# Hybrid attention block on one core: sparse value products from whole 32-bit operands, with three edits in the order of work beside them

## What is computed

```python
score = jnp.einsum('bqhs,bqh->bqs', jax.nn.relu(logits), wb)      # indexer, 4 heads
_, sel = lax.top_k(score, topk)                                    # 256 of the keys
sc = jnp.einsum('bqhd,bqkd->bhqk', qb, kg) * (dh ** -0.5)          # 8 heads of 64, one shared key head
p = jax.nn.softmax(sc, axis=-1)
return jnp.einsum('bhqk,bqkd->bqhd', p, vg)                        # the value products
```

## Time and profile before

| | |
|---|---|
| median of 3 runs | 2812.31 us (2811.92 to 2814.73) |
| the profiled execution | 2818.59 us, its span 2816.8 us |
| PE busy | 2528.1 us, 90% of the span, 13093 matmuls |
| DVE busy | 1786.0 us, 63% |
| ACT busy | 1372.1 us, 49% |
| POOL busy | 410.3 us, 15% |
| mean granted clock of PE | 0.972 of full speed |

### The profile page before, as it was taken

The page is one execution under the profiler, slowest core; times in us unless marked ns, Lnnn a source line. Parts: engine busy times, 40 slices in busy tenths (PEclk is TensorE's granted clock), DMA queues, the critical chain, the costliest instruction groups (busy, mean ns, idle before and its releaser), DMA issues.

```text
span 2816.8 us, 37280 instructions
## 1 busy us (share of the span) xinstructions
PE 2528.1 (90%) x13093; PEld 2095.4 (74%) x13093; DVE 1786.0 (63%) x3597; ACT 1372.1 (49%) x2768; POOL 410.3 (15%) x397
## 2 busy tenths in 40 slices
PE   5998999998999999999898999999878888878896
PEld 4776888776778888877677778887667777667785
DVE  6466676225767687227778878622778887777522
ACT  4455645344646444216657445522665673454511
POOL 5334353440000000100000000010000001000010
PEclk9999999999999999999999999999999999999998
DMA  5756584785343522664343511166324333000154
GB/s 162 227 176 213 170 282 150 252 278 183 115 162 119 173 76 68 209 209 155 115 143 104 165 60 53 46 217 206 137 83 149 105 108 132 23 31 31 38 179 165
DMA packets 172537, 399.36 MB, mean 142 GB/s; under 512 B 13760, under 2 KB 96704, under 8 KB 162368
## 3 DMA queue, kind: packets, MB, share of 16 engines
q1 hardware_dynamic: 172352, 396.96, 42.8%
HBM read 308.31 MB, written 88.60 MB: 141 GB/s over the span
## 4 chain that ended last, share of the span: by engine, by line
PE 51%; DVE 21%; ACT 15%; issue 10%; DMA 1%; POOL 1%; SPq 0%; DVEq 0%; ACTq 0%; POOLq 0%
PE bank L861 38%; PE TR L760 5%; PE PV L828 5%; ACT signs L1026 4%; ACT prob L991 3%; ACT prob L1001 3%; DVE ptL L1396 2%; ACT ptH L1015 2%; DVE prob L1355 2%; DVE nmx L1365 2%; DVE score L1617 2%; DVE zs L1427 1%; PE bank L771 1%; PE bank L772 1%; DVE flags L1543 1%
## 5 line engine op out<-in xcount | busy, mean ns | idle before, releaser
L861 PE MATMUL bank<-hH,pairs 128*128 128x512 f32 (+1 forms) x3584 | 1158.5, 393 | 21.0 <-DVE zs L1459 7.6
L861 PEld LDWEIGHTS bank<-hH,pairs 128*128 128x128 f32 x3584 | 679.3, 191 | 160.6 <-issue 22.2
L861 PE MATMUL bank<-hL,pairs 128*128 128x512 f32 (+2 forms) x1792 | 704.1, 393 | 0.0
L1026 ACT ACTIVATE signs<-score,bits 128x384 int8<-128x384 f32 (+7 forms) x256 | 335.8, 1312 | 214.5 <-DVE bits L1497 201.5
L1396 DVE TENSOR_TENSOR ptL<-TR,ptH 128x512 fp32r<-128x512 f32 (+1 forms) x384 | 256.9, 670 | 260.1 <-ACT ptH L1015 256.9
L861 PEld LDWEIGHTS bank<-hL,pairs 128*128 128x128 f32 (+1 forms) x1792 | 343.3, 192 | 65.2
L1015 ACT ACTIVATE ptH<-TR 128x512 fp32r<-128x512 f32 (+1 forms) x384 | 219.6, 576 | 333.6 <-PE TR L760 332.6
L1478 DVE TENSOR_SCALAR_CACHE_REDUCE above<-score,bits 128x256 uint8<-128x256 f32 (+10 forms) x280 | 348.1, 1243 | 9.5
L760 PE MATMUL TR<-identR,prob 128*128 128x128 f32 x1480 | 232.6, 279 | 101.0 <-ACT prob L1001 53.2
L760 PEld LDWEIGHTS TR<-identR,prob 128*128 128x128 f32 x1480 | 178.1, 142 | 178.4 <-ACT prob L1001 66.9
L1176 POOL TENSOR_TENSOR pairs<-raw,pairs 128x512 fp32r<-128x512 f32 x164 | 218.1, 1339 | 316.1 <-ACT pairs L960 315.9
(11 more groups left out here) (206 smaller groups left out, 3636.1 us busy)
## 6 DMA issues: line engine op xcount, KB each, us to landing
pairs<-w_split SPq DMA_DIRECT2D x444, 512.0 KB, 3.5
w_split<-pairs SPq DMA_DIRECT2D x74, 1024.0 KB, 4.9
raw<-in_w_in SPq DMA_DIRECT2D x106, 256.0 KB, 5.6
xs<-in_x SPq DMA_DIRECT2D x4, 2048.0 KB, 9.2
rows<-in_x SPq DMA_DIRECT2D x16, 512.0 KB, 5.2
out<-rows SPq DMA_DIRECT2D x4, 2048.0 KB, 7.5
table<-trig SPq DMA_DIRECT2D x48, 128.0 KB, 2.8
raw<-in_w_branch SPq DMA_DIRECT2D x24, 256.0 KB, 5.6
```

Source lines behind the costliest of these rows:

```text
L861: done = nc.tensor.matmul(PJ[st.u + half * up][0:min(st.width, P), 0:st.n_tok], lhs, rhs[:, row, 0:st.n_tok], start=(n % 12 == 0 and (up o ...
L1026: nc.scalar.activation(signs[:, 0:keys], score[:, tt, 0:keys], ACT.Sign, bias=thr.bitcast(F32)[:, tt:tt + 1], scale=-1.0, accum_out=cnt[:, ...
```

## The change

Branch B: `vS` holds whole float32 values and the transposed probabilities are copied once, by ACT, to float32 tiles `pt`. Each block of 128 keys gets one matmul with plain float32 operands in place of three with fp32r ones. DVE's subtraction is gone there, though DVE still waits at each tick for ACT's copy; ACT's copy frees the `TR` bank.

Order of work beside it: `due` now returns the first tick for the exponentials of the next C or A item. In the last group the first halves of the output rows are transposed and added between the last four output projections, the squares are taken row tile by row tile, and the scaled rows are stored in four DMAs. At the start ACT loads its table for squares with an early dummy square, waits only for the memory rows before it squares them, and takes their root before it splits the first weights. PSUM banks are tracked in one list (`take_bank`); which bank stands where does not change.

```diff
+    def take_turned(k=1, copied=None):
+
+        for i in range(k):
+            take("tr")
+            freed.append(event("tr_free") if copied is None else ("pt_hi", copied + i + 1))
+            take_bank("tr", freed[-1])
+        return n["tr"] - k
...
-    def finish_rows(g):
-        steps.append(Step("row_squares", g=g, tr=n["tr"]))
+            steps.append(Step("finish", g=g, tr=take_turned(), i=half, evac=last_out.evac))
+
+    def finish_last(g):
+
+        for tt in range(NT):
+            finish(g, 2 * tt + 1, 2 * tt + 2)
+            steps.append(Step("row_squares", g=g, tr=n["tr"], tt=tt, tiles=1))
         steps.append(Step("row_scale", g=g, tr=n["tr"]))
...
             it.groups = -(-it.keys // (2 * P)) if branch == "b" else 2
-            it.tr, it.p = take("tr", it.groups), take("p", it.groups)
+            it.p = take("p", it.groups)
+            it.tr = take_turned(it.groups, it.p if branch == "b" else None)
...
+            if m == KC // 2 - 1:
+                half_out = last_out
             if g + 1 < NG and m < KC - 1:
                 norm("x", g + 1, m + (m > 0), m + 2)
-    finish(NG - 1)
-    finish_rows(NG - 1)
-    return steps, every, pj_bank, s_bank, s_freed, x_freed, f_freed, swaps
+            elif g + 1 == NG and m >= KC // 2:
+                first = 2 * (m - KC // 2)
+                steps.append(Step("finish", g=g, tr=take_turned(), i=first, evac=half_out.evac))
+    finish_last(NG - 1)
...
-        vS = sb("vS", [P, SEQ // P * 2 * HD], F32R)
+        vS = sb("vS", [P, SEQ // P * HD])
...
+        pt = [sb(f"pt{i}", [P, T], offset=at_pt) for i, at_pt in enumerate((pt_at, pt_at + 2048, signs_at))]
...
             if st.branch != "b":
-                return [0 for _ in after], [ticks - 1]
+                return [0 for _ in after], [0]
...
-                        base, col, p = (2 * j + b) * P, slice(0, 256), slice(b * 256, (b + 1) * 256)
-                        vh, vl = vS[:, base:base + HD], vS[:, base + HD:base + P]
+                        base, col, p = (2 * j + b) * HD, slice(0, 256), slice(b * 256, (b + 1) * 256)
+                        v = vS[:, base:base + HD]
...
+                    if branch == "b":
+                        last = nc.tensor.matmul(bank[0:HD, col], v, pt[place_of(it, j)[0]][:, p], start=(j == 0 and b == 0),
+                                                stop=last_block, skip_group_check=True)
+                        continue
...
-                nc.scalar.activation(ptH[place][:, cols], TR[tr % 2][:, cols], ACT.Copy).then_inc(S["pt_hi"], 1)
+                to = (pt if branch == "b" else ptH)[place][:, cols]
+                nc.scalar.activation(to, TR[tr][:, cols], ACT.Copy).then_inc(S["pt_hi"], 1)
...
-                        act.wait_ge(S["small_in"], 16 * (NG + 3))
+                        act.wait_ge(S["consts"], 1)
+                        nc.scalar.activation(squared[:, 0:P], identR[:, :].bitcast(F32), ACT.Square).then_inc(S["squared"], 1)
+                        n_squares[0] += 1
...
+                elif st.kind == "scale":
+                    n_root += 1
+                    root(n_root, 0, source_rows(st)[0])
                     if st.source == "mem":
+                        act.wait_ge(S["small_in"], 16 * (NG + 3))
                         for half in range(4):
...
-                    parts = vS[:, un.g * T:(un.g + 1) * T].rearrange("p (t a c) -> p t a c", t=NT, a=2)
-                    hi, lo = parts[:, :, 0, :], parts[:, :, 1, :]
-                    link(nc.vector.tensor_copy(hi, cols[:, :, 0:HD]))
-                    last = TT(lo, cols[:, :, 0:HD], hi.bitcast(F32), ALU.subtract)
+                    parts = vS[:, un.g * NT * HD:(un.g + 1) * NT * HD].rearrange("p (t c) -> p t c", t=NT)
+                    last = nc.vector.tensor_copy(parts, cols[:, :, 0:HD])
...
+                if branch == "b":
+                    return
                 place, cols = place_of(it, j)[0], slice(0, width(it, j, branch))
-                TT(ptL[place][:, cols], TR[tr % 2][:, cols], ptH[place][:, cols].bitcast(F32), ALU.subtract).then_inc(S["tr_free"], 1)
+                TT(ptL[place][:, cols], TR[tr][:, cols], ptH[place][:, cols].bitcast(F32), ALU.subtract).then_inc(S["tr_free"], 1)
...
-                        last = STT(rows[:, t, :], rows[:, t, :], rstd[:, t:t + 1], gfin[:, :], ALU.mult, ALU.mult)
-                    last.then_inc(S["out_ready"], 1)
+                        STT(rows[:, t, :], rows[:, t, :], rstd[:, t:t + 1], gfin[:, :], ALU.mult, ALU.mult).then_inc(S["out_ready"], 1)```

How the instructions stand on PE in the last B stage, where a tick begins with the four transposes (`TR`) and the products of two ticks earlier follow (`PV`). Before:

```order
L760 MATMUL TR<-identR,prob 128x128 [waits tr_free,p_exp]
L760 MATMUL TR<-identR,prob 128x128 x3
L828 MATMUL PV<-ptH_91,vS 64x256 [waits tr_free,dve_pv]
L828 MATMUL PV<-ptH_91,vS 64x256
L828 MATMUL PV<-ptL_93,vS 64x256
L828 MATMUL PV<-ptH_91,vS 64x256 x2
```

More of the change, by code:

```diff
@@ L302, in order_of_work @@
     norm("mem", 0)
-    steps.append(Step("inverse", tr=take("tr")))
+    steps.append(Step("inverse", tr=take_turned()))
     prepare("x", 0)
@@ L603, in hybrid_block @@
         mVL = memkv[:, 3072:4096].rearrange("p (t n) -> p t n", t=2)
[L605 to L608, removed]
+        bank = [ctx.enter_context(nc.psum_tensor(name, [P, T], F32))
+                for name in ("bank0", "bank1", "bank2", "bank3", "bank4", "PV", "TR0", "TR1")]
+        PJ, SC, PV, TR = ([bank[i] for i, _ in banks_of[kind]] for kind in ("pj", "s", "pv", "tr"))
         names = """mem_rows_in x_in rows_in half_done small_in gfin_in raw_in0 raw_in1 pair_out0 pair_out1
@@ L639, in hybrid_block, with wait_turned @@
         spreads = [it.scale for st in steps if st.kind == "attention" for it in st.items if it.scale is not None]
+        def wait_turned(eng, last):
+            for name in ("tr_free", "pt_hi"):
+                upto = [value for engine, value in freed[:last + 1] if engine == name]
+                if upto:
+                    eng.wait_ge(S[name], upto[-1])
         def wait_free(eng, ring, index):
@@ L805, in products @@
             def products(it, branch, j):
[L807 to L810 removed]
+                if j == 0:
+                    wait_bank(banks_of["pv"], it.pv)
+                pe.wait_ge(freed_by[freed[it.tr + j][0]], freed[it.tr + j][1])
                 H, L = ptH[place_of(it, j)[0]], ptL[place_of(it, j)[0]]
[L812 removed]
+                bank = PV[it.pv]
                 end = j == it.groups - 1
@@ L962, in _, with squares @@
             n_squares = [0]
-            def squares(tiles, src):
-                for t in range(tiles):
+            def squares(tiles, src, first=0):
+                for t in range(first, first + tiles):
                     if n_squares[0]:
@@ L971, in squares, with root @@
                                          accum_out=ssq[:, t:t + 1]).then_inc(S["squared"], 1)
-            def root(n, tiles):
+            def root(n, first, tiles):
                 act.wait_ge(S["var_ready"], n)
-                nc.scalar.activation(rstd[:, 0:tiles], var[:, 0:tiles], ACT.Sqrt).then_inc(S["rooted"], 1)
+                nc.scalar.activation(rstd[:, first:first + tiles], var[:, first:first + tiles], ACT.Sqrt).then_inc(S["rooted"], 1)
             def exps(it, branch, head=0):
@@ L1152, in _ @@
                 elif st.kind == "row_squares":
-                    act.wait_ge(S["tr_free"], st.tr)
-                    squares(NT, rows)
+                    wait_turned(act, st.tr - 1)
+                    squares(st.tiles, rows, st.tt)
                 elif st.kind == "row_scale":
                     n_root += 1
-                    root(n_root, NT)
+                    root(n_root, 0, NT)
         @block.gpsimd
```

101 lines of the change are left out of this document (51 added, 50 removed).

## The result

The changed kernel takes 2911.64 us in the median of 4 runs (2908.67 to 2915.66), the kernel before 2812.11: a ratio of 1.0353, 95% interval 1.0335 to 1.0371. It is slower by 99.5 us, not by the 34 forecast, and outside the range given. The profiled execution has a span of 2912.2 us at a mean granted clock of 0.970.

A forecast was written before the change was run, and what follows sets the result against it. PE sets the pace in the first three B stages and waits a sixth of the last; an ACT-DVE loop paces C and A. +9 + 36 - 3.5 - 7 = +34.5 us on 2818.6, less 6.3: 2846, range 2799 to 2868.

The forecast's parts named there:

- Part 1: Value products of the B stages: one whole product takes 436 ns a block, 88 ns more than now, 48.3 us in all.
- well over 500: Sign against the forecast in the profile after: value products of the B stages at well over 500 ns a block.
- The rival of uncovered loads: B stages: loads of values are not covered, 137 ns more for each of 548 blocks, 75 us, time 2921; chance 0.08.
- Part 2: B stages: without DVE's subtractions idle time and clock loss come back, 28.4 + 6 us in the last, 3.6 and 1.5 before.
- The low end that I gave for them: B stages together: -10 us, the low end around +9, from the ends of the idle time alone.
- the forecast's own range: Whole kernel: 2830 to 2864, with 10 to 45 us idle kept in the last B stage, 464 ns a block; chance 0.58.
- Part 3: C and A stages: moved exponentials delay the bit search's loop through ACT and DVE, +36 us (C 16, A 19.5).
- Part 4: Start and end of the kernel: earlier squares and root give -3.5 us, earlier squares and split stores at the end -7.

## Why the prediction was wrong

The direction was right, the size was not: 99.5 us against 34.

- **Part 1 failed, in one step.** "A load of 64 columns can lie under the matmul before it, as the loads do in the rows." Those rows show split products beside split products and transpositions. The passes were right: 432 ns a block, forecast 436. The rule of the Trainium skill, FP8 and Floating Point Precision, TensorE Precision Notes, four passes, agrees with this trace in the sum, and a fourth of it, 108 ns, is a little under the 116 ns of a split product. But each group of whole products pays about 342 ns at its edges, 285 times: 97 us at full clock that the sum did not have. A group of two blocks so costs 1206 ns, 603 a block, the "well over 500" that the prediction named as its sign of being wrong. 105 us measured, 48.3 forecast; idle time that PE had anyway hid part of the price. The rival of uncovered loads was nearest: it charged 137 ns to every block, 75 us, where the edges take 342 a group, and so came near the measured total (2921). In that it is partly luck: its unit was wrong, and parts 2 and 3 were off as well. That the loads cause the edge is not shown.
- **Part 2 was too small.** The relief of DVE is worth 51 us, forecast 39.5. The last stage gave 27.7 (34.4 forecast), the first three 19.2 (5.1 forecast). The gaps of 2.9, 5.9 and 11.6 us were in the rows, and I let only 5.1 of these 20.4 us come back; 14 did, and 5 us of PE's busy time, which holds the way through the array, went with them. With part 1 the B stages make +50 us, not +9. The low end that I gave for them, -10, is also a wrong sum: 15 us more idle time given back makes +9 - 15 = -6. And in the forecast's own range, 45 us of idle kept and 464 ns a block together make 2846 + 20 + 15 = 2881, not 2864.
- **Part 3** had the sequence right, item by item, and C's 16 and A's 19.5 for g = 1 to 3 (measured 17.3 and 19.1 in the stages). It left out the A stage of g = 0 (+7.0) because its counts are short; they are 384 and 512 columns there, and with 128 the loss is 2.1. And it left out what arises behind the C stages, 5.9 us. 51 us alone, forecast 36. For C the cause was named wrongly: the length of the bit counts plays no part, the copy behind waiting exponentials is enough. For A the loop through the counts is shown: with short ones the move costs nothing in g = 1 to 3.
- **Part 4** was right: -13, forecast -10.5; in the trace -7.3 at the end (forecast -7) and -2.7 at the start of the first C stage (forecast -3.5).

The range failed because its upper end left out the only case in which something beside the passes was charged to the whole products, at 0.08. What causes the edge inside TensorE stays open: the runs show where it falls, that the number of products does not change it, and that the kind of neighbour changes only its last term.

## What to carry to other kernels

Price an operation that the trace does not show by its body and by its edges: count how often the kernel changes from one kind of matmul to the other, not only how many there are. Count the edge to its end: here the second matmul behind the group was still late. Where PE's busy share is near one, the small gaps that are left can still all come back, and a little of the busy time with them. And before an instruction is moved ahead in an in-order queue, look for how long its own input is late; what stands behind it pays that wait, and whether it matters is decided by the slack of the stage.

## What the runs showed of the hardware

- A matmul with both operands plain float32 stands in the trace as two records of 216 ns for 256 columns, each with its own load, 432 ns a block; a split (fp32r) product of the same size is 116 ns (kernel before).
- Going into such products costs 94 ns from a float32 transposition and about 95 from an fp32r product, the second record another 51, going out 93 (to either). The matmul behind that one is late once more, by 104 ns between fp32r products and by 56 between transpositions (run with the products first). A group of 2, 4 or 8 records pays the same. Between transpositions and fp32r products there is no such cost (28 + 199 ns for steps of 109 + 116).
- The loads show it: PE's loads stop running ahead at these places (0.17 and 0.39 us idle for "issue" in the tick at 1101 us of the changed kernel).
